# Two transformer blocks on one core: the first phase's pool chain, norm sums, bias table and first unit rearranged

## What is computed

```python
h = rmsnorm(x, norm_mix_g)
proj = h @ w_in                       # 2048 -> 4096: 1024 pool, 3 x 1024 q, k, v
u, qkv = proj[..., :1024], proj[..., 1024:]
# pool mixer: 4 groups of 256 columns, windows w = 2, 4, 8, 16
mean = (c - shifted(c, w)) / minimum(pos, w)      # c = cumsum(u) over tokens
y = einsum('bsgc,gcf->bsgf', mean - u, pool_w) * pool_scale
y_pool = rmsnorm(y, pool_out_norm_g)
y_attn = rmsnorm(dilated_attention(q, k, v), attn_out_norm_g)   # 8 heads
x = x + concat(y_pool, y_attn) @ w_out
```

## Time and profile before

| | us |
|---|---|
| median of three runs | 2662.48 |
| profiled execution, its own span | 2662.0 |
| TensorE busy | 2625.2 |
| VectorE, ScalarE, GpSimd busy | 1927.2, 1255.0, 287.2 |
| TensorE idle ahead of its first product | 8.44 |

### The profile page before, as it was taken

The page is one execution under the profiler, slowest core; times in us unless marked ns, Lnnn a source line. Parts: engine busy times, 40 slices in busy tenths (PEclk is TensorE's granted clock), DMA queues, the critical chain, the costliest instruction groups (busy, mean ns, idle before and its releaser), DMA issues.

```text
span 2662.0 us, 35344 instructions
## 1 busy us (share of the span) xinstructions
PE 2625.2 (99%) x12718; PEld 2184.3 (82%) x12718; DVE 1927.2 (72%) x2332; ACT 1255.0 (47%) x1545; POOL 287.2 (11%) x322
## 2 busy tenths in 40 slices
PE   8999999999999999999999999999999999999998
PEld 8997888888888887887877777888788888888886
DVE  5786677788788779776676888787755555555687
ACT  6445544444444446455455444444544444444443
POOL 0041041424142000062000000000000000000000
PEclk9999999999999999999999999999999999999999
DMA  8665777887788876846544665698565555555784
GB/s 305 225 207 191 232 263 252 282 274 266 254 278 280 268 259 225 278 166 217 169 164 154 238 206 194 221 310 303 185 198 190 191 191 191 191 190 189 261 304 161
DMA packets 281133, 606.97 MB, mean 228 GB/s; under 512 B 19472, under 2 KB 20688, under 8 KB 279104
## 3 DMA queue, kind: packets, MB, share of 16 engines
q1 hardware_dynamic: 276704, 579.41, 64.8%
q0 software_dynamic: 4320, 26.13, 2.7%
HBM read 594.17 MB, written 11.29 MB: 227 GB/s over the span
## 4 chain that ended last, share of the span: by engine, by line
PE 92%; DVE 3%; issue 1%; ACT 1%; DMA 1%; POOL 1%; DVEq 0%; SPq 0%; ACTq 0%; POOLq 0%
PE ps L603 90%; PE ps L727 1%; DVE arena L1950 1%; DVE w_lo L1955 1%; DMA w_raw<-in_w_up 1%; ACT w_hi L1285 1%; DMA w_raw<-in_w_in 1%; PE ps L754 0%; PE ps L717 0%; DVE x L1970 0%; DVE arena L2896 0%; PE ps L738 0%; DVE w_lo L2404 0%; PE ps L1192 0%; ACT arena L1564 0%
## 5 line engine op out<-in xcount | busy, mean ns | idle before, releaser
L1285 ACT ACTIVATE w_hi<-w_raw 128x1024 fp32r<-128x1024 f32 (+1 forms) x897 | 947.8, 1058 | 1330.0 <-PE ps L603 1251.5
L1955 DVE TENSOR_TENSOR w_lo<-w_raw,w_hi 128x1024 fp32r<-128x1024 f32 x809 | 1012.5, 1254 | 628.0 <-ACT w_hi L1285 624.5
L603 PE MATMUL ps<-w_hi,hop_part 128*128 128x512 f32 x4264 | 1343.5, 392 | 3.4 <-DVE hop_part L2307 1.2
L603 PEld LDWEIGHTS ps<-w_hi,hop_part 128*128 128x128 f32 x4264 | 801.1, 188 | 182.7 <-issue 11.0
L603 PE MATMUL ps<-w_lo,hop_part 128*128 128x512 f32 x2132 | 830.4, 389 | 0.0
L603 PEld LDWEIGHTS ps<-w_lo,hop_part 128*128 128x128 f32 x2132 | 400.7, 188 | 80.6
L603 PE MATMUL ps<-w_hi,hid_hi_part 128*128 128x512 f32 x992 | 388.6, 392 | 0.0
L603 PE MATMUL ps<-w_hi,hid_lo_part 128*128 128x512 f32 x992 | 386.3, 389 | 0.0
L603 PE MATMUL ps<-w_lo,hid_hi_part 128*128 128x512 f32 x992 | 385.9, 389 | 0.0
L603 PE MATMUL ps<-hop_part,w_hi 128*128 128x256 f32 (+1 forms) x1312 | 325.4, 333 | 8.4 <-ACT w_hi L1285 8.4
L1950 DVE SCALAR_TENSOR_TENSOR arena<-arena,cs 128x768 f32<-128x768 f32 x240 | 255.8, 1066 | 0.0
(11 more groups left out here) (321 smaller groups left out, 1373.4 us busy)
## 6 DMA issues: line engine op xcount, KB each, us to landing
arena<-in_ada_w SPq DMA_DIRECT2D x256, 384.0 KB, 4.7
w_raw<-in_ffn_w_in SPq DMA_DIRECT2D x176, 512.0 KB, 3.5
w_raw<-in_w_up SPq DMA_DIRECT2D x128, 512.0 KB, 4.0
w_raw<-in_w_down SPq DMA_DIRECT2D x128, 512.0 KB, 4.8
w_raw<-in_w_gate SPq DMA_DIRECT2D x128, 512.0 KB, 4.2
w_raw<-in_w_in SPq DMA_DIRECT2D x88, 512.0 KB, 3.7
w_raw<-in_ffn_w_out SPq DMA_DIRECT2D x88, 512.0 KB, 3.5
w_raw<-in_w_out SPq DMA_DIRECT2D x64, 512.0 KB, 5.0
```

Source lines behind the costliest of these rows:

```text
L603: return nc.tensor.matmul(o, w, r, start=start, stop=stop, skip_group_check=True)
L1285: return nc.scalar.activation(o, i, ACT.Copy, scale=scale)
L1955: V.tensor_tensor(w_lo[:, j % LEAD, :, 0:cols], w_raw[:, j % RAW, :, 0:cols], w_hi[:, j % LEAD, :, 0:cols].bitcast(F32), ALU.subtract).the ...
```

## The change

At the start SyncE loads only the first 16 vector columns before the weights and the rest after unit 3 (these too are counted in `tokens_in`). Unit 0 is loaded, copied by ScalarE and multiplied in two halves of 128 rows. ScalarE makes `cs` (a Silu) after the split of unit 11 instead of that of unit 8. VectorE copies the inverse and drains the first chunk ahead of the split of unit 18 instead of behind it. The bias table is one product with 4 output rows, one ScalarE copy of 4 partitions, and a DMA that reads each of the 4 rows 128 times. In the pool chain the first 16 tokens are scaled in place by a constant that holds `w / min(pos, w)`; side tile, subtract and copy go. The squares of each norm are added by GpSimd, in pairs of tiles and then to two tiles; TensorE sums two. The first four squares of norm 1 move to unit 58, those left stay at unit 60, and `norm_sum(2)` goes from after output unit 3 to after output unit 4.

```diff
@@ -239,7 +239,7 @@
     for g, w in enumerate(POOL_WINDOWS):
-        c["poolfix"][:, g * POOL_PAD:(g + 1) * POOL_PAD] = 1.0 / np.minimum(np.arange(POOL_PAD) + 1, w)
+        c["poolfix"][:, g * POOL_PAD:(g + 1) * POOL_PAD] = w / np.minimum(np.arange(POOL_PAD) + 1, w)
     for ii in range(4):
@@ -482,11 +482,16 @@
         load_x(0)
-        sp.dma_start(vecs[:], columns).then_inc(sem["vec_in"], 16)
-        for q in range(RAW):
-            load(0, q, w_in[q, :, :, IN_ORDER[0] * COLS:(IN_ORDER[0] + 1) * COLS], cond=False)
+        sp.dma_start(vecs[:, 0:KT], columns[:, 0:KT]).then_inc(sem["vec_in"], 16)
+        first = slice(IN_ORDER[0] * COLS, (IN_ORDER[0] + 1) * COLS)
+        sp.dma_start(w_raw[:, 0, 0], w_in[0, :, 0, first]).then_inc(sem["first_in"], 16)
+        sp.dma_start(w_raw[:, 0, 1], w_in[0, :, 1, first]).then_inc(raw_landed[0], 16)
+        load_x(1)
+        for q in range(1, RAW):
+            load(0, q, w_in[q, :, :, first], cond=False)
             if q < 3:
                 load_x(q + 1)
+        sp.dma_start(vecs[:, KT:], columns[:, KT:]).then_inc(sem["tokens_in"], 16)
         for g in range(2):
@@ -621,13 +626,20 @@
-            pe.wait_ge(sem["hi_ready"], R_IN * 8 + (j + 1))
             slot = j % LEAD
-            for f in range(FT):
-                o, cols = place(f)
-                for k in range(UK):
+
+            def high(k):
+                for f in range(FT):
+                    o, cols = place(f)
                     mm(o, w_hi[:, slot, k, cols], hop_hi[:, UK * j + k], start=j == 0 and k == 0 and f % 2 == 0, stop=False)
                     mm(o, w_hi[:, slot, k, cols], hop_lo[:, UK * j + k], start=False, stop=False)
+
+            if j == 0:
+                pe.wait_ge(sem["first_hi"], 1)
+                high(0)
+            pe.wait_ge(sem["hi_ready"], R_IN * 8 + (j + 1))
+            for k in range(1 if j == 0 else 0, UK):
+                high(k)
             pe.wait_ge(sem["lo_ready"], R_IN * 8 + (j + 1))
@@ -697,13 +709,11 @@
-        def norm_sum(n, groups):
-
-            sq = T(NORM_SQ[n], NORM_TILES[n])
-            for g in groups:
-                pe.wait_ge(sem["sq_ready"], 2 * (n - 1) + g + 1)
-                for k in range(4 * g, 4 * g + 4):
-                    m = mm(NORM_BANK, ones[:], sq[:, k], start=k == 0, stop=k == NORM_TILES[n] - 1)
+        def norm_sum(n):
+
+            pe.wait_ge(sem["sq_summed"], n)
+            for k in range(2):
+                m = mm(NORM_BANK, ones[:], T(NORM_SQ[n] + k), start=k == 0, stop=k == 1)
             m.then_inc(sem["sum_ready"], 1)
@@ -775,15 +785,13 @@
                     m = mm(PS[4][:, t * P:(t + 1) * P], ones[:], span(46, t * P, P))
-                m.then_inc(sem["inv_psum"], 1)
+                m.then_inc(sem["early_psum"], 1)
             if u == 17:
...
                 pe.wait_ge(sem["const_in"], 16)
-                pe.wait_ge(sem["bias_rows_ready"], 1)
-                for h in range(BR_HEADS):
-                    m = mm(PS[4 + h][:, 0:384], span(50, h * P, P)[BROWS, :], C("rowsel", n=384)[BROWS, :])
-                m.then_inc(sem["bias_psum"], 1)
+                pe.wait_ge(sem["small_in"], 16 * N_SMALL)
+                mm(PS[4][0:BR_HEADS, 0:384], bias_table, C("rowsel", n=384)[BROWS, :]).then_inc(sem["early_psum"], 1)
             for h in range(HEADS):
@@ -814,7 +822,7 @@
                 pe.wait_ge(sem["pool_ready"], 4)
-                norm_sum(1, range(2))
+                norm_sum(1)
@@ -835,8 +843,8 @@
                 m.then_inc(sem["a_out_psum"], 1)
-            if u == 3:
-                norm_sum(2, range(2))
+            if u == 4:
+                norm_sum(2)
             for c in range(3):
@@ -1372,29 +1380,32 @@
             m.then_inc(sem["hop_hi"], 2)
-            if b < LEAD:
+            if b == 0:
+                act.wait_ge(sem["first_in"], 16)
+                copy(w_hi[:, 0, 0], w_raw[:, 0, 0]).then_inc(sem["first_hi"], 1)
+                act.wait_ge(raw_landed[0], 16)
+                act.wait_ge(sem["first_hi"], 1)
+                copy(w_hi[:, 0, 1], w_raw[:, 0, 1]).then_inc(sem["hi_ready"], 1)
+            elif b < LEAD:
                 split(0, b, first=True)
         def first_mixer(u):
-            if u == 4:
-                nc.scalar.activation(cs[:], vec("c_2", 0, KT), ACT.Silu).then_inc(sem["cs_ready"], 1)
             if 7 <= u < 11:
                 if u == 7:
-                    act.wait_ge(sem["tokens_in"], 64)
+                    act.wait_ge(sem["tokens_in"], 80)
+                    nc.scalar.activation(cs[:], vec("c_2", 0, KT), ACT.Silu).then_inc(sem["cs_ready"], 1)
                 m = token_square(SUM_X, u - 7, x_tok, (0, 4, 12, 38)[u - 7])
...
             if u == 17:
-                act.wait_ge(sem["bias_psum"], 1)
-                for h in range(BR_HEADS):
-                    m = copy(span(32, h * 384, 384), PS[4 + h][:, 0:384])
-                m.then_inc(sem["bias_copied"], 1)
+                act.wait_ge(sem["early_psum"], 2)
+                copy(span(32, 0, 384)[0:BR_HEADS, :], PS[4][0:BR_HEADS, 0:384]).then_inc(sem["bias_copied"], 1)
             if u == 15:
                 act.wait_ge(sem["lam_sums"], 1)
-                nc.scalar.activation(lam_s[:, 2:4], lam_s[:, 0:2], ACT.Exp).then_inc(sem["lam_exps"], 1)
-                nc.scalar.activation(s5v[:, DT], s5v[:, 15], ACT.Exp).then_inc(sem["s_dt"], 1)
+                nc.scalar.activation(lam_s[:, 2:4], lam_s[:, 0:2], ACT.Exp)
+                nc.scalar.activation(s5v[:, DT], s5v[:, 15], ACT.Exp).then_inc(sem["exps_ready"], 1)
             if u == 21:
@@ -1425,10 +1436,12 @@
                         m.then_inc(sem["pool_ready"], 1)
+            if u == 58:
+                act.wait_ge(sem["pool_ready"], 2)
+                squares(1, 1, 0)
             if u == 60:
                 act.wait_ge(sem["pool_ready"], 4)
-                for g in range(2):
-                    squares(1, g, 0)
+                squares(1, 0, 0)
@@ -2039,19 +2052,15 @@
-        def bias_rows():
+        def lambda_sums():
             dve.wait_ge(sem["small_in"], 16 * N_SMALL)
-            for h in range(BR_HEADS):
-                m = V.tensor_scalar(span(50, h * P, P)[BROWS, :], ones[BROWS, :],
-                                    bias_table[:, h:h + 1], None, ALU.mult)
-            m.then_inc(sem["bias_rows_ready"], 1)
             then(V.tensor_tensor(lam_prod, lam[:, 0::2, :], lam[:, 1::2, :], ALU.mult))
...
-            dve.wait_ge(sem["lam_exps"], 1)
+            dve.wait_ge(sem["exps_ready"], 1)
             then(V.tensor_tensor(lam_s[:, 4:5], lam_s[:, 3:4], lam_s[:, 2:3], ALU.subtract))
@@ -2133,7 +2142,7 @@
-            dve.wait_ge(sem["s_dt"], 1)
+            dve.wait_ge(sem["exps_ready"], 1)
             then(V.tensor_tensor(v(MAG), v(DT), are, ALU.mult))
@@ -2194,6 +2203,10 @@
         for j in range(8 * UA):
+            if j == 14:
+                dve.wait_ge(sem["early_psum"], 1)
+                then(V.tensor_copy(inv0, PS[4][:, 0:S]))
+                scaled_chunk(0)
             split(R_IN, j + LEAD)
@@ -2209,12 +2222,8 @@
                 dve.wait_ge(sem["cs_ready"], 1)
-            if j == 14:
-                dve.wait_ge(sem["inv_psum"], 1)
-                then(V.tensor_copy(inv0, PS[4][:, 0:S]))
-                scaled_chunk(0)
             if j == 15:
-                bias_rows()
+                lambda_sums()
             if j == 17:
@@ -2963,15 +2972,14 @@
         pool.wait_ge(sem["bias_copied"], 1)
-        pool.dma_start(bias_scratch[:].rearrange("h p j -> p h j"),
-                       span(32, 0, BR_HEADS * 384).rearrange("p (h j) -> p h j", h=BR_HEADS)).then_inc(sem["scratch_out"], 16)
+        pool.dma_start(bias_scratch[:], span(32, 0, 384)[0:BR_HEADS, :].unsqueeze(1).to_broadcast([BR_HEADS, P, 384])
+                       ).then_inc(sem["scratch_out"], 16)
         pool.wait_ge(sem["scratch_out"], 16)
...
         bufs = [span(40, 2 * (pad + S) * i, 2 * (pad + S)).rearrange("p (a b) -> p a b", a=2) for i in range(2)]
-        head = span(55, 0, 2 * pad).rearrange("p (a b) -> p a b", a=2)
         for b in bufs:
@@ -2989,15 +2997,30 @@
             scale = C("poolfix", lo=g * pad, n=pad).unsqueeze(1).to_broadcast([P, 2, pad])
-            then(G.tensor_tensor(head, tail[:, :, pad:2 * pad], scale, ALU.mult))
-            then(G.tensor_tensor(head, head, u[:, :, 0:pad], ALU.subtract))
+            then(G.tensor_tensor(tail[:, :, pad:2 * pad], tail[:, :, pad:2 * pad], scale, ALU.mult))
             then(G.tensor_scalar(tail[:, :, pad:], tail[:, :, pad:], 1.0 / w, None, ALU.mult))
-            then(G.tensor_tensor(u, tail[:, :, pad:], u, ALU.subtract))
-            then(G.tensor_copy(u[:, :, 0:pad], head))
-            pool.sem_inc(sem["pooled"], 1)
-
+            G.tensor_tensor(u, tail[:, :, pad:], u, ALU.subtract).then_inc(sem["pooled"], 1)
+            pool.wait_ge(sem["pooled"], POOL_ORDER.index(g) + 1)
+
+        def square_pair(n, count, g):
+
```

(15 more changed lines are left out.)

8 lines of the change are left out of this document (4 added, 4 removed).

## The result

The changed kernel is slower. Its median is 2686.06 us (2683.07 to 2686.82, four runs) beside 2662.95 us for the kernel before on the same chip: a ratio of 1.0083, interval 1.0071 to 1.0095. The forecast was 2657.2 us with a range up to 2667.0, and the time lies 19 us above its upper end. The profiled execution took 2683.07 us, its span is 2681.3. Instead of 5.3 us less it is 23.1 us more.

What follows compares the result with a forecast made beforehand. TensorE bounds the kernel, busy 2625.2 of 2662.0 us. Gains 1.5 + 0.8 + 2.1 + 1.2 + 1.8 + 0.25 - 0.55 = 7.1, less 1.8 for one clock fall, give 5.3: 2657.2 us, range 2654.5 to 2667.

Steps and rivals of the forecast that it cites:

- The bias write: Table write to DRAM, now from 4 partitions: lands in 4.8 to 28 us and by itself costs nothing.
- (c): Rival: the slow table write starves the weight loads; 1 to 8 us show plus a clock fall, 2660 to 2667.5; chance 0.20.
- Length: Within (c): the table write lasts 28 us, four engines together getting one engine's 28 GB/s, 0.22 us per 1.5 KB piece.
- Pace: Within (c): weight pieces queue behind table pieces, 4.7 us per unit against 2.8; six units come instead of ten, 11 us short.
- (d): Rival: at both norms GpSimd's adds collide fully with VectorE's splits, 2 us each, with clock loss; 1.5 gained, 2661; chance 0.05.
- The start: First product 1.2 to 2.5 us earlier; cover of 1.37 us at unit 10 limits the gain to 1.5 (0.8 to 2.0).
- The early inverse and the bias products: Inverse copied before a weight split removes a 0.8 us TensorE wait; one bias product instead of four gains 2.1.
- The pool chain: Last pool product 1.2 us earlier (0.7 to 1.6), wait 2.4 becomes 1.2; no clock fall behind it, 1.8 more gained.
- First norm: Two products instead of eight remove 2.45 us; a new wait of 2.2 for GpSimd's adds leaves 0.25 gained.
- Second norm: Sum one unit later, waiting 0 to 0.6; output unit 8 starts 0.55 us later (0.2 to 1.0) after 2.9 idle.
- The sum: All terms together: 7.1 us gained, less 1.8 for one clock fall, 5.3 us, giving 2657.2 us.
- I expect one of the two: Of the new stalls of 2.2 us (first norm) and 2.9 us (output unit 8), one causes a clock fall costing 1.8.

Runs made afterwards that it cites:

- e6: The changed kernel with the slow table write cut into two halves, the second issued only when the splits reach unit 44: 2670.81 us (one run).
- e3: The changed kernel with the bias table's rows spread by VectorE over 128 partitions and written from all of them: 2660.21 us, ratio 0.9988.
- e10: The kernel of e12 with the start as in the kernel before (columns in one load, first unit whole, Silu at unit 4): 2654.87 us.
- e12: Second measurement of e3 with five products per norm (GpSimd adds only the four early squares, second sum at unit 3): 2653.75 us, ratio 0.9963.
- e7: e3 with both norms as before (eight products each, second sum at output unit 3, no GpSimd adds): 2657.16 us, ratio 0.9979.
- e9: e3 with only the second norm as before (eight products at output unit 3, no GpSimd adds for it): 2657.56 us, ratio 0.9977.
- e1: The changed kernel with the bias table as before (four products, four copies, write from 128 partitions): 2661.27 us, ratio 0.9990.
- e4: The changed kernel with the table write reading four rows four partitions apart (0, 4, 8, 12), each 128 times: 2660.58 us (one run).
- e5: The changed kernel with the table write reading 16 neighbouring partitions, four copies of each row, each read 32 times: 2657.63 us (one run).
- e11: The kernel of e12 with the pool chain on GpSimd as in the kernel before (subtract and copy back again): 2654.68 us.

## Why the prediction was wrong, step by step

**The bias write** is the step that failed: "By itself it costs nothing; what it does to weight loads is a rival below." The forecast put the write at nothing; it cost 24.6 us. The rival, (c), named the mechanism and the sign, and had a chance of 0.20; its terms for the length, the pace and the price were too small. The last of the prediction's own signs of being wrong came true: ScalarE waited 24.53 us for weights, up to 101.79.
- Length: 28 us was taken from four partitions that share one engine's 28 GB/s, four engines with 0.22 us for a piece of 1.5 KB. The pieces were 172 of mostly 4.6 KB at 0.71 us, which is 0.24 per 1.5 KB: 30.3 us on each of four engines. The rate was about right; the landing came at 37.2.
- Pace: this term was far off. Each weight piece queues behind a piece of the table, as (c) had it, but behind one of 0.71 us, not of 0.22. From its first to its last piece the write lasted 33.4 us, so each of the four engines had 3.1 us, a tenth of its time, for everything else, where the same stretch before wanted 0.67 to 0.87 of it (the rows of windows above). A weight tile is usable only when its last piece is in. So not six of ten tiles came, but hardly more than one: by the landings in the trace a weight tile at 73.23 and a modulation tile at 89.92, and the next weight tile at 101.77, just behind the write. In time that is, as an estimate, 33.4 x (1 − 0.09/0.77) = 29.5 us short, where 11 were reckoned. The Trainium skill, "DMA: Bandwidth & Descriptors", section on queues, rings and completion order, says that an engine takes turns between its queues by the packet. The trace agrees as far as it can be counted: if the pieces of a tile (of 2 KB, and of 3 KB for modulation) are spread evenly over 16 engines, these three tiles are 16 + 8 + 16 = 40 pieces on each, beside 43 of the table's.
- Lead: some 10 us were assumed; 29.5 less the 22.1 shown is 7.4, and the first portion of e6, reckoned in the same way, gives about 10. Right in size.
- Price: (c) gave 1 to 8 us, at worst 11 and a clock fall. It was 22.1 and 2.5, as TensorE started again at half clock. (By its own terms (c) adds up to 2667.0 and 2670.0 where 2667.5 and 2672 stand, and (d) to 1.3 us gained, not 1.5; nothing hangs on it.)
- The point from which it decides, "over some 15 us", was about right: 17.2 us showed 1.0, 19.6 us 2.7 and 5.4.

The chance was too low too. Two facts of the case spoke for (c), the 768 KB and the four source partitions, and against it stood only that nothing in the trace was large enough to tell. The pieces of the write before are in its trace (0.18 us each); that their size, not 1.5 KB, times the rate of the new source is a turn of 0.7 us could have been worked out, and would have made (c) the forecast or put the upper end near 2690 (an estimate).

**The start**: forecast 1.5 (0.8 to 2.0). The first product was at 5.90, at the early end, but the cover ran out already at units 3 and 4 (waits of 0.62 and 1.05), not at unit 10. At the product that sums the token norm the changed kernel is 54.22 − 53.59 = 0.63 us ahead, e3 0.11, and e10 and e12 differ by 0.36. So most of the 1.5 was not there; by the medians it is anything from nothing to 1.1. The term was too large because it took the cover at unit 10 for the smallest one.

**The early inverse and the bias products**: forecast 0.8 + 2.1 = 2.9. The wait of 0.8 is gone. From the sum at 54.22 to the first pool product at 194.13 the kernel before needs 139.91 us; e3 needs 190.57 − 54.11 = 136.46 and e12 189.24 − 52.77 = 136.47. So 3.4 us, a little more.

**The pool chain**: forecast a wait of 1.2, bounded by a saving of 0.7 to 1.6; it is 1.86, a saving of 0.55. Two rows of e12 show where the rest went (GpSimd, VectorE):

```profile
199.80 2.07 POOL L3006 TENSOR_TENSOR arena<-arena 128x512 f32<-128x512 f32 x1
...
199.52 1.23 DVE L1971 TENSOR_TENSOR w_lo<-w_raw,w_hi 128x1024 fp32r<-128x1024 f32 x1 [1.49 <-ACT w_hi L1296]
```

The last subtract of the chain takes 2.07 us, and 1.26 without company (205.73 in the kernel before). Coming earlier, it has slid under VectorE's weight split; before, the split (at 204.42) met the step ahead of it, which took 1.49 us there and here. The steps were subtracted right, their new neighbour was not looked up. The clock stayed full behind the wait in the changed kernel, as forecast.

**First norm**: forecast 2.45 removed, a wait of 2.2, 0.25 gained. The wait is 2.31 in every trace with GpSimd's adds, and e7 and e9 show no difference. The size is right, in part by luck: the adds took 1.30 and 1.26 us in the changed kernel, not 1.04, and where the second met a split it was the split, begun later (235.93), that was stretched, to 2.06 us.

**Second norm**: forecast 0.55 lost, and a hole of 2.9 ahead of unit 8. From the product behind the first sum to unit 8 the kernel before takes 253.24 − 219.56 = 33.68 us, e3 248.33 − 213.78 = 34.55: 0.87 lost, with a hole of 2.71, within the bounds of 0.2 to 1.0. But the changed kernel itself takes 273.14 − 237.81 = 35.33 us, 1.65 lost: its second add took 2.13 us and the sum waited 0.89, where 0 to 0.6 was forecast. So did e1 and e4 (2.13 and 2.18, waits of 1.07 and 1.09), while in e3, e5 and e6 the add took 1.28 or 1.29 and the wait was 0.23 at the most. This is the second half of rival (d). Right in kind, the bounds too narrow; with the clock falls it comes to most of the 3 us between e3 and e7.

**The sum** without the table: forecast 5.3, or 7.1 less 1.8 for each clock fall. e3 gains 2.9 in the median: the start gave less than 1.5, the pool wait 0.55 instead of 1.2, and the second norm took 0.9 to 1.7 instead of 0.55. Its executions lie between 2655.7 and 2662.3, on the forecast's own scale from no fall to more than two. "I expect one of the two" was the step with the least behind it.

## What to carry over

A DMA that reads a few neighbouring rows many times was slow here, and a slow DMA is not private: the loads that use the same engines are late until it ends. Before a write is made cheaper for the compute engines, multiply its bytes by the rate of its source rows and compare that with the lead of the loads around it; here a VectorE copy that spread the rows kept what the rest of the change gained (2660.21, and 2661.27 with the old table). Work removed from the critical engine just ahead of a chain is worth what the chain leaves of it, so reduce only the part that is ready early (five products beat both two and eight).

## What the runs showed of the hardware

- The same 768 KB took 37.2, 17.2, 10.6 and 7.0 us to read from 4 neighbouring rows, 4 rows four apart, 16 neighbouring rows and 128 rows; a piece of 4608 bytes took 0.7 us from 4 or 16 neighbours and 0.18 from the others.
- Issuing slows down too: SyncE needed 4.58 us for one load and 12.91 for three during the slow write, where it had taken 0.34 for one.
- The clock does not follow from the length of a wait alone. In the traced executions it fell behind 1 of 11 waits of 1.86 us (in e5), 3 of 7 of 2.31, 2 of 3 of 2.4 and 5 of 6 of 2.7. In e1 it fell once at 65 us with no wait ahead, behind the four bias products. One fall costs 1.7 to 1.8 us (1.66 in e11, 1.84 before). The prediction took a fall behind a wait of 2.4 us as settled; in these runs it is a chance, and it shows as a spread of the executions of e3, 6.6 us, where e7's is 3.2.
- An add or subtract of 128x512 on GpSimd took 1.04 to 1.30 us alone or nearly so. In two places where they met, the later one was stretched: a subtract begun 0.3 us behind a split of VectorE took 2.07 us, and a split begun 0.3 us behind an add 2.06 instead of 1.23.
